# Rows first in one queue: reordering the loads and the first blocks of a transformer kernel on Trainium2

## What is computed

```python
mod_x = (jax.nn.silu(c) @ w_ada[l] + b_ada[l])[:, None, :]
mod_c = (jax.nn.silu(c_ctx) @ w_ada[l] + b_ada[l])[None, None, :]
sh_a, sc_a, g_a, sh_m, sc_m, g_m = jnp.split(mod_x, N_MOD, axis=-1)
csh_a, csc_a, cg_a, csh_m, csc_m, cg_m = jnp.split(mod_c, N_MOD, axis=-1)
hx = _modulate(_rmsnorm(x, norm_attn[l]), sh_a, sc_a)
hc = _modulate(_rmsnorm(cx, norm_attn[l]), csh_a, csc_a)
qa, ka, va, qb, kb, vb, ga, gb = proj(hx)       # columns of h @ w_in
cqa, cka, cva, cqb, ckb, cvb, cga, cgb = proj(hc)
```

## Time and profile before

| what | value |
|---|---|
| median of 3 runs | 1895.02 us (1891.53 to 1895.54) |
| the profiled execution's own time | 1893.38 us |
| its span, first to last instruction | 1891.5 us |
| PE busy | 1793.1 us (95%) |
| DVE / ACT busy | 669.7 us (35%) / 577.0 us (31%) |
| HBM read | 560.58 MB |
| mean granted TensorE clock | 0.994 of full |

### The profile page before, as it was taken

One profiled execution on the slowest core, in us unless ns is written; L12 is line 12 of the kernel. 1 busy time (PEld: TensorE's weight loads), 2 busy tenths in 40 slices (PEclk: granted clock), 3 DMA queues, 4 the chain that ended last, 5 costly groups with the idle time before them and its releaser, 6 DMA issues.

```text
span 1891.5 us, 24352 instructions
## 1 busy us (share of the span) xinstructions
PE 1793.1 (95%) x10246; PEld 1089.5 (58%) x10246; DVE 669.7 (35%) x1211; ACT 577.0 (31%) x1044; POOL 20.1 (1%) x59
## 2 busy tenths in 40 slices
PE   5999999999999999999999999989999999989999
PEld 4987787333333333323233232358799997779998
DVE  2654664111111111111111111144654555645454
ACT  4455564101100110101101011044554445555443
POOL 0010010000000000000000000000000000000000
PEclk9999999999999999999999999999999999999999
DMA  8745446999999999999999999975346464425550
GB/s 307 258 156 190 173 179 273 411 429 426 428 427 428 427 427 428 427 428 428 427 428 427 427 428 427 428 286 177 134 151 205 139 220 153 134 90 182 175 200 24
DMA packets 122048, 563.25 MB, mean 298 GB/s; under 512 B 7216, under 2 KB 53424, under 8 KB 97360
## 3 DMA queue, kind: packets, MB, share of 16 engines
q1 hardware_dynamic: 121104, 558.70, 73.9%
q10 hardware_dynamic: 832, 2.95, 0.4%
HBM read 560.58 MB, written 1.05 MB: 297 GB/s over the span
## 4 chain that ended last, share of the span: by engine, by line
PE 74%; DMA 20%; DVE 3%; ACT 2%; issue 1%; SPq 0%; ACTq 0%; DVEq 0%
DMA ring<-in_w_up 18%; PE ps L1084 14%; PE ps L652 12%; PE ps L653 12%; PE ps L654 12%; PE ps L1107 8%; PE ps L1042 2%; PE ps L1022 2%; DMA ring<-in_w_ada 1%; PE ps L970 1%; PE ps L664 1%; PE ps L1003 1%; DMA ring<-in_w_in 1%; PE ps L757 1%; DVE part L1980 1%
## 5 line engine op out<-in xcount | busy, mean ns | idle before, releaser
L652 PE MATMUL ps<-part,part 128*128 128x256 f32 (+2 forms) x1592 | 512.8, 322 | 7.5 <-DVE part L1980 5.1
L653 PE MATMUL ps<-part,part 128*128 128x256 f32 (+2 forms) x1592 | 502.6, 316 | 0.0
L654 PE MATMUL ps<-part,part 128*128 128x256 f32 (+2 forms) x1592 | 502.3, 316 | 0.0
L1084 PE MATMUL ps<-ring,arena 128*64 128x512 f32 x1536 | 340.6, 595 | 18.6 <-DMA ring<-in_w_up 17.6
L1980 DVE TENSOR_TENSOR part<-ring,part 128x1024 fp32r<-128x1024 f32 (+2 forms) x299 | 313.1, 1088 | 125.1 <-ACT part L1439 124.4
L652 PEld LDWEIGHTS ps<-part,part 128*128 128x128 f32 (+1 forms) x1592 | 304.9, 192 | 41.6 <-issue 13.2
L654 PEld LDWEIGHTS ps<-part,part 128*128 128x128 f32 (+1 forms) x1592 | 304.5, 191 | 19.4
L653 PEld LDWEIGHTS ps<-part,part 128*128 128x128 f32 (+1 forms) x1592 | 305.0, 192 | 17.1
L1439 ACT ACTIVATE part<-ring 128x1024 fp32r<-128x1024 f32 (+2 forms) x299 | 271.8, 947 | 33.8 <-PE ps L654 18.7
L1084 PEld LDWEIGHTS ps<-ring,arena 128*64 128x64 f32 x1536 | 105.8, 137 | 250.3 <-issue 208.2
L1977 DVE TENSOR_SCALAR arena<-ps 128x512 f32<-128x512 f32 x64 | 44.2, 691 | 438.6 <-PE ps L1084 438.6
(11 more groups left out here) (250 smaller groups left out, 1121.9 us busy)
## 6 DMA issues: line engine op xcount, KB each, us to landing
ring<-in_w_gate SPq DMA_DIRECT2D x48, 2048.0 KB, 31.6
ring<-in_w_up SPq DMA_DIRECT2D x48, 2048.0 KB, 32.3
ring<-in_w_down SPq DMA_DIRECT2D x48, 2048.0 KB, 35.3
ring<-in_ffn_w_in SPq DMA_DIRECT2D x44, 1024.0 KB, 7.8
arena<-in_w_gate SPq DMA_DIRECT2D x16, 2048.0 KB, 31.6
arena<-in_w_up SPq DMA_DIRECT2D x16, 2048.0 KB, 32.3
arena<-in_w_down SPq DMA_DIRECT2D x16, 2048.0 KB, 35.4
ring<-in_w_ada SPq DMA_DIRECT2D x12, 2048.0 KB, 10.4
```

Source lines behind the costliest of these rows:

```text
L652: e.matmul(out, x[0], y[0], start=first, stop=False, skip_group_check=True)
L653: e.matmul(out, x[0], y[1], start=False, stop=False, skip_group_check=True)
L654: return e.matmul(out, x[1], y[0], start=False, stop=last, skip_group_check=True)
L1084: i = e.matmul(PS[p + r][CAP * h:CAP * h + CAP, :], xg[:, k0 + k, :], W(w)[:, k, 512 * h:512 * h + 512], start=False, stop=k0 == 4 and k = ...
```

## The change

1. SP issues all early transfers: `par`, `X` and `con` first, then ada 0, ada 2, the first half (features 0 to 511) of qa, the context rows, the first half of kva, ada 1, ada 3, the second halves of kva and qa, then kb as before. The second halves have semaphores of their own and wait for nothing.
2. The query blocks of the first half (qa0 p0, qa1 p0) come ahead of kva p0.
3. The tokens are turned before ada 0. The context is scaled by ScalarE in place (two activations of 1024 columns) and turned by plain transposes behind block 1, into banks 6, 7, 0 and 1; ada 1 and ada 3 come behind it.
4. TensorE gets 56 transposes of the identity into bank 6 that nobody reads, in groups of 10, 5, 16, 5 and 20 between the first steps.
5. `high_a`, `low_a`, `u_low` and `raw` of ScalarE and VectorE are put in the order that the new blocks need.

```diff
-        for key in (("ada", 0, 0), ("ada", 2, 1), ("in", "kva"), ("ada", 1, 0), ("ada", 3, 1), ("in", "qa"), ("in", "kb"), ("ada", 4, 1),
+        for key in (("ada", 0, 0), ("ada", 2, 1), ("in", "qa", 0), ("in", "kva", 0), ("ada", 1, 0), ("ada", 3, 1), ("in", "kva", 1),
+                    ("in", "qa", 1), ("in", "kb"), ("ada", 4, 1),
...
-        a_order = [("kva", 0), ("qa0", 0), ("qa1", 0), ("kva", 1), ("qa0", 1), ("qa1", 1)]
+        a_order = [("qa0", 0), ("qa1", 0), ("kva", 0), ("kva", 1), ("qa0", 1), ("qa1", 1)]
...
         def sync_program(e):
+            early = PCOL["b_gate"]
+            e.dma_start(par[:, 0:early], A["par"][:, 0:early]).then_inc(*s_par.up())
+            e.dma_start(X[:, :, :], A["x"].rearrange("(q p) n -> p q n", p=128)).then_inc(*s_x[0].up())
+            e.dma_start(con[:, :], A["con"]).then_inc(*s_con.up())
...
+                if key == ("in", "qa", 0):
+                    e.dma_start(a.cx, A["ctx"].rearrange("(q p) n -> p q n", p=128)).then_inc(*s_x[1].up())
...
+            def unit_turns(n):
+                for _ in range(n):
+                    e.transpose(PS[6][:, 0:128], C("ident"), C("ident"))
+
+            e.wait_ge(*s_con.of())
+            unit_turns(10)
...
             e.wait_ge(*s_silu.of())
             ada(0, 4)
-
-
-            e.wait_ge(*s_con.of())
-            for who, rows in enumerate((X, a.cx)):
+            unit_turns(5)
+            ada_columns(0, 4, a.rows[0])
+            unit_turns(16)
+            ada(2, 5)
+            unit_turns(5)
+            ada_columns(2, 5, a.rows[2])
+            unit_turns(20)
+
+            def turn_context():
+
                 for q in range(2):
-                    e.wait_ge(*s_diag.of("first", who, q))
+                    e.wait_ge(*s_cscaled.of(q))
                     for j in range(2):
-                        if who:
-                            e.wait_ge(*(s_urawd if j else s_uraw).of(0, q))
+                        if q:
+                            e.wait_ge(*(s_urawd if j else s_uraw).of(0, 0))
                         for k in range(4):
...
+                            at = 512 * j + 128 * k
+                            i = e.transpose(PS[(6, 7, 0, 1)[2 * q + j]][:, 128 * k:128 * k + 128], a.cx[:, q, at:at + 128], C("ident"))
+                        i.then_inc(*s_ut.up("first", 1, q, j))
...
-                if t == 0:
+                if t == 1:
+                    turn_context()
+                    e.wait_ge(*s_uraw.of(1, 0))
                     ada(1, 6)
+                    e.wait_ge(*s_urawd.of(1, 0))
                     ada(3, 7)
-                if t == 1:
...
             ada_row(0, 4, a.rows[0])
+            ada_row(2, 5, a.rows[2])
             high_a(0)
-            ada_row(2, 5, a.rows[2])
-            raw(1, 0)
             for p in (0, 1):
                 u_high(0, p)
-            raw(1, 1)
-            for p in (0, 1):
-                context_mod(p)
-                u_high(1, p)
+            high_a(1)
+            first_root(1, a.cx)
+            e.wait_ge(*s_xss.of("first", 1))
+            for q in range(2):
+                e.activation(a.cx[:, q, :], a.cx[:, q, :], ACT.Copy, scale=a.xs[1][:, 4 + q:5 + q]).then_inc(*s_cscaled.up(q))
+            high_a(2)
+            for q in range(2):
+                raw(1, q)
+            context_mod(0)
+            u_high(1, 0)
             ada_row(1, 6, a.rows[1])
-            high_a(1)
+            context_mod(1)
+            u_high(1, 1)
             ada_row(3, 7, a.rows[3])
-            high_a(2)
             high_a(3)
```

More of the change, by code:

```diff
@@ L297, in build @@
         a.yd = [a.rowx[:, 128 * v:128 * v + 128] for v in range(8)]
-        a.first_diag = [[a.rowx[:, 256 * who + 128 * q:256 * who + 128 * q + 128] for q in range(2)] for who in range(2)]
+        a.first_diag = [a.rowx[:, 128 * q:128 * q + 128] for q in range(2)]
         a.diag = [a.table[:, 0, i, :, :].rearrange("p q d -> p (q d)") for i in range(2)]
@@ L673, in ada_columns @@
                 i.then_inc(*s_col.up(s))
+            def unit_turns(n):
[4 more added lines that the diff above has]
+            for q in range(2):
+                e.wait_ge(*s_diag.of("first", q))
+                for j in range(2):
+                    for k in range(4):
+                        i = e.matmul(PS[2 * q + j][:, 128 * k:128 * k + 128], X[:, q, 512 * j + 128 * k:512 * j + 128 * k + 128],
+                                     a.first_diag[q], start=True, stop=True, skip_group_check=True)
+                    i.then_inc(*s_ut.up("first", 0, q, j))
             e.wait_ge(*s_silu.of())
             ada(0, 4)
[L679 to L680 removed]
+            unit_turns(5)
[6 more added lines that the diff above has]
+            def turn_context():
                 for q in range(2):
[L682 removed]
+                    e.wait_ge(*s_cscaled.of(q))
                     for j in range(2):
[L684 to L685 removed]
+                        if q:
+                            e.wait_ge(*(s_urawd if j else s_uraw).of(0, 0))
                         for k in range(4):
[L687 to L693, removed]
+                            at = 512 * j + 128 * k
+                            i = e.transpose(PS[(6, 7, 0, 1)[2 * q + j]][:, 128 * k:128 * k + 128], a.cx[:, q, at:at + 128], C("ident"))
+                        i.then_inc(*s_ut.up("first", 1, q, j))
             def bank_free(name):
@@ L1452, in scalar_program, with first_root @@
             e.preload_act_table(ACT.Sqrt)
-            for who, rows in enumerate((X, a.cx)):
+            def first_root(who, rows):
                 e.wait_ge(*s_x[who].of())
-                if who == 0:
-                    e.wait_ge(*s_con.of())
                 for q in range(2):
@@ L1464, in raw @@
                 e.wait_ge(*s_ut.of("first", who, q, 0))
-                copy(a.uT[:, who, 0:4, 128 * q:128 * q + 128], PS[2 * q].rearrange("p (k n) -> p k n", k=4)).then_inc(*s_uraw.up(who, q))
+                bank = (6, 0)[q] if who else 2 * q
+                copy(a.uT[:, who, 0:4, 128 * q:128 * q + 128], PS[bank].rearrange("p (k n) -> p k n", k=4)).then_inc(*s_uraw.up(who, q))
+            first_root(0, X)
             for q in range(2):
@@ L2033, in vector_program @@
                 if g == 0:
-                    raw(1, 0)
+                    low_a(0)
                 u_low(0, 2 * g)
+                u_low(0, 2 * g + 1)
                 if g == 0:
-                    raw(1, 1)
-                u_low(0, 2 * g + 1)
+                    low_a(1)
+                    first_inverse(1)
+                    low_a(2)
+                    for q in range(2):
+                        raw(1, q)
                 for p in (2 * g, 2 * g + 1):
@@ L2041, in vector_program @@
                 if g == 0:
-                    for t in range(1, 4):
-                        low_a(t)
+                    low_a(3)
             for t in range(4, 8):
```

56 lines of the change are left out of this document (32 added, 24 removed).

## The result

The changed kernel took 1884.82 us (median of 18 runs, 1881.98 to 1889.96), beside 1891.49 us for the kernel before (18 runs, 1887.35 to 1895.65). The ratio is 0.9965, interval 0.9957 to 0.9973: **6.7 us faster**, 5.1 to 8.1. The profiled execution of the changed kernel took 1882.83 us.

What follows compares the result with a forecast made beforehand. PE's chain was taken to bound the time through stage a, the experts' weights 340 to 1220 us. Ada 4 4.9 us earlier, all reaching the end, made 1893.38 into 1888.4, or 1890.0 against the median 1895.02; range 1885.5 to 1895.0.

Steps and rivals of the forecast that it cites:

- the head: Start of the kernel up to ada 4: earlier loads and reordered PE work were to end it 4.9 us earlier.
- Landing of ada 2: Ada 2's slab, fourth in the new transfer order, was to land at 19.0 us by summed bytes.
- tokens' turn: Transposing the tokens on PE before ada 0, partly at half clock, was to end at 15.35 us.
- context's turn: 16 plain transposes behind block 1 were to take 1.8 us instead of 3.8, a gain of 2.0.
- ScalarE's last row copy: End of ScalarE's chain ahead of columns 3, put at 41.05 us, with 0.4 us lost at the columns.
- ada 4: Ada product behind blocks 4 and 5, to start at 59.2 to 59.3 us instead of 64.17.
- Dips of the clock: Low-clock stretches of PE, as at 176.6 us: 3.4 us long, costing 1.5 each, either way.
- From 66 us on the order is unchanged: Everything behind 66 us was to start earlier by the head's gain, so all 4.9 us reach the end.
- the base: Time subtracted from: profiled execution 1893.38 us, 1.64 under the median, and against the median of 1895.02 it gave 1890.0.
- the unit turns don't hold the clock: Rival, 20%: transposes count for nothing in the clock gate early in the kernel; gain 2.2 us, 1892.8.
- ScalarE's chain: Rival, 12%: ScalarE, nearly gapless from 27 to 50 us, delays blocks by 2 us; gain 2.9, 1892.1.
- The filler at the low clock: Rival, 8%: unit turns at 1.2 GHz hold up the ada products behind them; 6 us slower, 1901.

Runs made afterwards that it cites:

- without the sixteen: The changed kernel without its group of 16 unit transposes, which stands ahead of ada 2's product: 1884.59 us, ratio 0.9963 to the kernel before.
- without the twenty: The changed kernel without its last group of 20 unit transposes, in the wait ahead of block 0: 1885.22 us, ratio 0.9967 to the kernel before.
- the second group: The changed kernel run again with no edit, beside the kernel before: 1885.25 us, ratio 0.9964.
- the second profile of the kernel before: Profile from running the kernel before once more with no edit: 1894.97 us, ratio 1.0008.

## Why the prediction was right and where it was wrong

**Right: the head.** Landing of ada 2 at 19.0 (18.9, without the sixteen), tokens' turn to 15.35 (15.5), block 0 at 28.4 (28.35), context's turn 1.8 (1.9), ScalarE's last row copy to 41.05 (40.16 + 0.58), kb issued at 43.5 (43.3), ada 4 at 59.2 (59.15). Over three profiles each it is 64.3 before and 59.5 after: 4.8 us. Two terms at the start were off and cancelled, which is luck: PE started at 7.9 and not 8.4, and the clock rose at 13.6 and not 12.2, so the tokens' turn took 5.43 us where the sum had 4.65. Ada 3 landed at 37.6 and not 37.0. The first full clock came at 12.6 to 15.1 us in the three profiles of the changed kernel, and the constants landed at 7.7 to 9.5; ada 4 moves by up to 1.9 us with them, so that 59.15 for 59.2 is closer than the sum could be.

**Wrong, first: "Dips of the clock, as at 176.6, stand in other places or not at all: 3.4 us at spacing 0.21 instead of 0.12 costs 1.5, either way."** I took the sum of them as zero. It isn't: the change brings 56 unit turns, and the mean clock rises from 0.9932 to 0.9948 in the same group of runs. The turns alone, well placed in the old kernel, give 4.2 us (2.3 to 6.1), of which 1.1 is ada 6's transfer; the new order alone (no turns) gives 2.5 (0.6 to 4.4) though its ada 4 is 5.2 us earlier, as its clock is lower still (0.9912). That these two add up to the 6.7 measured says little, since each is uncertain by 1.9; that both the order and the turns have a part is shown. I counted the turns by what they cost and asked only whether the clock would fall because of the change, not how often it fell in the kernel before: the one profile that I had is the only one of three with a full clock through the head, and the earlier trace rows showed the wait of 3.38 us without a fall. I read one execution as the rule. Most of what the turns save is not in the head, where I looked for dips, but behind it.

**Wrong, second: "From 66 us on the order is unchanged, so the whole 4.9 reaches the end."** The head start was still 5.0 when ada 6 was issued (86.49 against 91.52), but 1.1 to 1.4 us were added there, at the one wait of the earlier trace rows that was for a transfer. I had read that wait as hanging on the issue alone.

**Wrong, third: the base.** I subtracted from the median of three runs, 1895.02; larger groups give 1891.49 to 1893.66. Of the miss of 5.2 us (1890.0 against 1884.8) some 3.5 are this (1895.02 against 1891.49), which is the luck of three runs, and 1.7 the two steps above (5.0 predicted as gain, 6.7 measured, 5.1 to 8.1).

**The rivals.** That the unit turns don't hold the clock (20%) is refuted: with them no fall in the head in seven profiles, without them six in seven. The rule of the Trainium skill, page "TensorE: Matmul & The Clock Gate", Part 4, that a transpose doesn't count as work for the clock gate the way a matmul does, doesn't hold in this kernel: in 24.40 to 28.35 us PE did 20 fp32 transposes and then waited 1.53 us, at clock 1.00, where the same stretch without the transposes fell (0.76 without the twenty, 0.63 without all). The measurement decides. It is one of holding the clock; no run has transposes alone in front of a rise. ScalarE's chain (12%) swallowed nothing: 0.15 us of wait at the columns, none behind. The filler at the low clock (8%) didn't come about: the clock rose at 12.6 to 15.1 us.

**Open.** How the turns of the head make the later falls (169 to 178, 235 to 241, 311 to 321, 1630 us) rarer, and which of the groups do it: without the twenty the profile has no fall between 60 and 1240 us, without the sixteen one, and neither time is told apart from the changed kernel's. How much time the clock gave back was not separated either. By mean clock it is at most 3.0 us; with the head's 4.8 and ada 6's 1.1 that would be 8.9, more than the 7.5 between the means of the second group. So part of the low clock must lie where it costs less than half its length, as the fall at 28.0 us did ahead of the wait for qa (ada 4 at 63.55 with it, 64.17 without).

## What to carry to other kernels

Where a matrix engine waits in short pieces, cheap work without a reader in the waits can be worth as much as a better order of the loads (here 4.2 us against 2.5 in a kernel of 1890), and without it half of what the better order gains in the head is lost again behind it (5.2 us at ada 4, 2.5 in the total). Where it has to stand is less clear than I would like: in the old order the turns gained only when some stood in the thin stretch itself (1888.8 us against 1891.9), in the new order leaving out just those cost 1.2 us, inside the noise, and leaving out all cost 4.5. A single profile doesn't tell how often the clock falls: look at the mean clock of all runs, or at three profiles, before a stretch is called safe. When loads are moved forward, move the instructions that wait for them on the in-order engines as well, or the one that lands late holds up those behind it.

## What the runs showed of the hardware that I had not expected

- Plain fp32 transposes keep the granted clock at full (0 falls in the head in 7 profiles, against 6 in 7), and kernels that have them in the head show less low clock long after it (3.4 us against 10.9 between 60 and 1240 us).
- Ten of them at the start took 2.40 us at the low clock and twenty 2.38 at the full one.
- A stretch that is busy can be followed by a fall: in the second profile of the kernel before PE was busy 2.43 of 3.20 us from 25.0 to 28.2, with the columns (two-column matmuls) and then the context's turn, and the clock fell at 28.0. A wait of nothing at all for 3.38 us had no fall, one of 3.18 us had.
- A 16 KB fetch of code on one DMA engine, 1.07 us long, goes with 1.1 us more for a 2 MB transfer (13.7 against 12.6 us from its issue to the next one); 34 or more extra transposes on PE earlier in the program move it elsewhere.
- A fall at the router's matmuls of 64 columns lasts 10.2 us (in four of fourteen profiles: three of the five without any turn, one of the nine with turns).
